# Hybrid decoder layer on one core: another order for weight splits, bank copies and the loading of hidden sums in the MLP

## The reference

```
x = x + gate1 * (concat(attention, retention) @ w_out)
h = rms_norm(x, norm2_g) * (1.0 + scale2) + shift2
x = x + gate2 * (square(relu(h @ w_mlp1)) @ w_mlp2)
```

## Time and profile before

| | |
|---|---|
| median of 3 runs | 1140.83 us |
| profiled execution | 1139.11 us, of which the span is 1137.3 us |
| TensorE busy in the span | 1093.8 us (96%) |
| VectorE busy | 762.2 us (67%) |
| ScalarE busy | 442.0 us (39%) |
| GpSimd busy | 244.0 us (21%) |
| mean granted TensorE clock | 0.985 of full |

### The profile page before, as it was taken

The page is one execution under the profiler, slowest core; times in us unless marked ns, Lnnn a source line. Parts: engine busy times, 40 slices in busy tenths (PEclk is TensorE's granted clock), DMA queues, the critical chain, the costliest instruction groups (busy, mean ns, idle before and its releaser), DMA issues. The chain is left out here.

```text
span 1137.3 us, 14052 instructions
## 1 busy us (share of the span) xinstructions
PE 1093.8 (96%) x5210; PEld 884.9 (78%) x5210; DVE 762.2 (67%) x1206; ACT 442.0 (39%) x746; POOL 244.0 (21%) x219
## 2 busy tenths in 40 slices
PE   5999999999999999997999999999899999999998
PEld 4578877777778988775888888888678788787786
DVE  5673556564546767897676767667986957848752
ACT  6342333354444334662232323233523514426231
POOL 2011000000001105312222323233323223232231
PEclk9899999999999999998999999999999999999999
DMA  9958433332013013103535353537626345336205
GB/s 272 275 163 265 130 123 101 122 101 90 28 38 122 28 33 108 38 0 130 193 113 191 114 190 116 187 120 224 257 95 233 135 148 191 99 117 222 74 1 148
DMA packets 150932, 151.71 MB, mean 133 GB/s; under 512 B 14116, under 2 KB 124880, under 8 KB 147280
## 3 DMA queue, kind: packets, MB, share of 16 engines
q1 hardware_dynamic: 142800, 122.45, 33.4%
q0 software_dynamic: 8064, 28.36, 7.6%
HBM read 113.04 MB, written 37.75 MB: 133 GB/s over the span
## 5 line engine op out<-in xcount | busy, mean ns | idle before, releaser
L739 PE MATMUL ps<-cmb_hi,wm_hi 128*128 128x512 f32 x880 | 350.0, 398 | 23.2 <-DVE wm_lo L1904 8.1
L740 PE MATMUL ps<-cmb_lo,wm_hi 128*128 128x512 f32 x880 | 346.2, 393 | 0.0
L741 PE MATMUL ps<-cmb_hi,wm_lo 128*128 128x512 f32 x880 | 346.1, 393 | 0.0
L739 PEld LDWEIGHTS ps<-cmb_hi,wm_hi 128*128 128x128 f32 x880 | 167.6, 190 | 65.7 <-issue 12.4
L741 PEld LDWEIGHTS ps<-cmb_hi,wm_lo 128*128 128x128 f32 x880 | 167.4, 190 | 35.7
L740 PEld LDWEIGHTS ps<-cmb_lo,wm_hi 128*128 128x128 f32 x880 | 167.7, 191 | 34.6 <-issue 0.5
L739 PE MATMUL ps<-act_hi,w_hi 128*128 128x512 f32 x400 | 162.3, 406 | 3.0 <-DVE act_lo L1682 3.0
L740 PE MATMUL ps<-act_lo,w_hi 128*128 128x512 f32 x400 | 157.1, 393 | 0.0
L741 PE MATMUL ps<-act_hi,w_lo 128*128 128x512 f32 x400 | 157.0, 392 | 0.0
L1392 ACT ACTIVATE wm_hi<-wm_f 128x512 fp32r<-128x512 f32 x128 | 77.2, 627 | 204.7 <-POOL wm_f L709 158.0
L2155 DVE SCALAR_TENSOR_TENSOR x1t<-ps,ada,x1t 128x512 f32<-128x512 f32 x112 | 83.5, 746 | 79.8 <-PE ps L741 79.8
(11 more groups left out here) (200 smaller groups left out, 1406.4 us busy)
## 6 DMA issues: line engine op xcount, KB each, us to landing
raw<-in_w_mlp_dram SPq DMA_DIRECT2D x128, 256.0 KB, 3.9
cmb_f<-h_spill SPq DMA_DIRECT2D x22, 1024.0 KB, 5.3
wada<-in_w_ada_dram POOLq DMA_DIRECT2D x32, 512.0 KB, 5.0
h_spill<-stage SPq DMA_DIRECT2D x16, 768.0 KB, 6.5
w_raw<-in_w_in_dram SPq DMA_DIRECT2D x18, 512.0 KB, 3.9
ada_rows<-in_w_ada_dram SPq DMA_DIRECT2D x16, 512.0 KB, 7.3
h_spill<-stage SPq DMA_DIRECT2D x32, 256.0 KB, 3.2
h_spill<-stage SPq DMA_DIRECT2D x16, 512.0 KB, 6.7
```

Source lines behind the costliest of these rows:

```text
L739: pe.matmul(bank, wh, hi, start=first, stop=False, skip_group_check=onto)
L740: pe.matmul(bank, wh, lo, start=False, stop=False, skip_group_check=onto)
L741: return pe.matmul(bank, wl, hi, start=False, stop=last, skip_group_check=onto)
```

## The change

Nothing is added to or taken from the arithmetic. Instructions are put in another order in four places.

- **First pairs, VectorE.** The splits of pair 1 (S1, A22, S2) stand ahead of, or between, `c12(0)` and the squares of pair 0. `c11(2)` with its square moves from pair 1 to pair 2, behind `last_sum(1)`. The splits A11 and A12 of pair 3 stand directly behind `last_sum(0)`.
- **First pairs, ScalarE and SyncE.** `weight_hi(1, A22)` moves into pair 0. In pair 1 the hi parts of pair 3's A11 and A12 and of pair 2's S3 and S1 stand ahead of `e2(1)`; `e1(2)` moves into pair 2. The load of pair 3's weights waits for the sums of pair 1. The store of b11 of pair 2 moves one pair later, behind that pair's load and two other stores.
- **Change of phase.** T1, T3 and T2 of chunk 0 are loaded before the last sums are stored. On VectorE `e25(15)` and `c22(15)` stand ahead of the split of B11, `last_sum(14)` behind it, and T2 and T1 are split in pair 16. `e2(15)` moves behind the hi parts of T2 and T1.
- **Chunk ends.** In the last pair of a chunk VectorE adds the last product and the first of the next pair before it splits T1. The first pair of a chunk has one order for all four chunks: T3, additions 1 and 2, S4, B22, addition 3, A22, addition 4, NT4, and only then A11 of the next pair.

```diff
@@ -80,19 +80,19 @@
     if AHEAD <= _a < 2 * PAIRS and _w != PAIRS - 1:
         SPLITS += [(_a, A11), (_a, A12)]
     if _w + 1 < 2 * PAIRS:
-        SPLITS += [(_w + 1, _i) for _i in (S3, S1, S2, S4, A22)]
+        SPLITS += [(_w + 1, _i) for _i in ((S3, S1, S2, S4, A22) if _w else (S3, S1, A22, S2, S4))]
...
-UP_SUMS = [("e25", 0), ("c22", 0), ("c11", 1), ("c11", 0), ("c12", 0), ("e25", 1), ("c22", 1), ("c21", 0), ("c11", 2),
-           ("c12", 1), ("c21", 1)]
-SQUARES = [("b22", 0), ("b11", 0), ("b12", 0), ("b21", 0), ("b11", 1), ("b11", 2), ("b22", 1), ("b12", 1)]
+UP_SUMS = [("e25", 0), ("c22", 0), ("c11", 1), ("c11", 0), ("c12", 0), ("e25", 1), ("c22", 1), ("c21", 0), ("c12", 1),
+           ("c21", 1), ("c11", 2)]
+SQUARES = [("b22", 0), ("b11", 0), ("b12", 0), ("b21", 0), ("b22", 1), ("b11", 1), ("b12", 1)]
...
-    SQUARES += [("b21", _p - 1)] + [("b11", _p + 1)] * _more + [("b22", _p), ("b12", _p)]
+    SQUARES += [("b21", _p - 1)] + [("b11", 2)] * (_p == 2) + [("b11", _p + 1)] * _more + [("b22", _p), ("b12", _p)]
 SQUARES += [("b21", PAIRS - 1)]
...
-FIRST_LOADS = (B11, B21, T1, T2, T3, B22, NT4)
...
-        def loads_of(q):
-            return FIRST_LOADS if q == 0 else tuple(range(7))
-
         def piece(q, i, part):
 
-            return 14 * q + 2 * loads_of(q).index(i) + part + 1
+            return 14 * q + 2 * i + part + 1
 
...
@@ -581,8 +577,15 @@
                     sp.wait_ge(s, 16 * CHUNK_PAIRS * (q + 1))
 
             for p in range(PAIRS):
+                if p == PAIRS - 1:
+                    load_in_place(0, T1)
                 sp.wait_ge(s_wlm, SPLIT[p, A22])
+                if p == 1:
+                    sp.wait_ge(s_s, 4 * p + 4)
                 load_pair(p + 2)
+                if p == PAIRS - 1:
+                    load_in_place(0, T3)
+                    load_in_place(0, T2)
                 if p:
                     store_sums(p - 1)
                     store_b21(p - 1)
@@ -591,7 +594,11 @@
                     store_b11(0)
                     continue
                 if p == 1:
+                    store_b22(1)
                     store_b11(1)
+                    continue
+                if p == 2:
+                    store_b11(2)
                 if p + 1 < PAIRS:
                     store_b11(p + 1)
                     if p == PAIRS - 2:
@@ -599,7 +606,7 @@
                         load_in_place(0, B11)
                         load_in_place(0, B21)
                     store_b22(p)
-            for i in FIRST_LOADS[2:]:
+            for i in (B22, NT4):
                 load_in_place(0, i)
 
             for w in range(PAIRS, 2 * PAIRS):
@@ -1501,29 +1508,30 @@
             e2(0)
 
             for p in range(PAIRS):
-                if p == 1:
-                    weight_hi(1, A22)
-                    e5(1)
-                    e2(1)
-                    e1(2)
-                elif p:
+                if p >= 2:
                     weight_hi(p, A22)
+                    if p == 2:
+                        e1(2)
                     if p + 1 < PAIRS:
                         e1(p + 1)
+                if p:
                     e5(p)
                 if p and p + 1 < PAIRS:
                     weight_hi(p + 2, A11)
                     weight_hi(p + 2, A12)
                 weight_hi(p + 1, S3)
                 weight_hi(p + 1, S1)
-                if p >= 2:
+                if p == 0:
+                    weight_hi(1, A22)
+                elif p + 1 < PAIRS:
                     e2(p)
-                if p == PAIRS - 1:
-                    combination_hi(0, T1)
                 weight_hi(p + 1, S2)
                 if p == PAIRS - 1:
                     combination_hi(0, T2)
                 weight_hi(p + 1, S4)
+                if p == PAIRS - 1:
+                    combination_hi(0, T1)
+                    e2(p)
                 if p == PAIRS - 2:
                     combination_hi(0, B11)
                     combination_hi(0, B21)
@@ -2073,30 +2081,28 @@
             weight_lo(1, S3)
             c11(1)
             c11(0)
+            weight_lo(1, S1)
+            weight_lo(1, A22)
             c12(0)
             squared(ST_B22, n_c22(0))
             squared(0, n_c11(0))
+            weight_lo(1, S2)
             squared(ST_T3, n_c12(0))
-            weight_lo(1, S1)
             hidden_sums(0)
-            weight_lo(1, S2)
             weight_lo(1, S4)
-            weight_lo(1, A22)
             e25(1)
             c22(1)
             c21(0)
             squared(ST_B21, n_c21(0))
             last_sum(0)
-            squared(1, n_c11(1))
-            c11(2)
-            squared(0, n_c11(2))
-            squared(ST_B22, n_c22(1))
             weight_lo(3, A11)
             weight_lo(3, A12)
+            squared(ST_B22, n_c22(1))
+            squared(1, n_c11(1))
             weight_lo(2, S3)
+            weight_lo(2, S1)
             c12(1)
             squared(ST_T3, n_c12(1))
-            weight_lo(2, S1)
             weight_lo(2, S2)
             c21(1)
 
@@ -2104,15 +2110,16 @@
                 weight_lo(p, S4)
                 weight_lo(p, A22)
                 hidden_sums(p - 1)
-                squared(ST_B21, n_c21(p - 1))
-                last_sum(p - 1)
                 if p + 1 < PAIRS:
+                    squared(ST_B21, n_c21(p - 1))
+                    last_sum(p - 1)
+                    if p == 2:
+                        c11(2)
+                        squared(0, n_c11(2))
                     c11(p + 1)
                     squared((p + 1) % 2, n_c11(p + 1))
                     weight_lo(p + 2, A11)
                     weight_lo(p + 2, A12)
-                else:
-                    both_lo(0, B11)
                 e25(p)
                 c22(p)
                 if p + 1 < PAIRS:
@@ -2121,8 +2128,10 @@
                     c12(p)
                     squared(ST_T3, n_c12(p))
                 else:
+                    both_lo(0, B11)
+                    squared(ST_B21, n_c21(p - 1))
+                    last_sum(p - 1)
                     both_lo(0, B21)
-                    both_lo(0, T1)
                     weight_lo(p + 1, S3)
                 weight_lo(p + 1, S1)
                 weight_lo(p + 1, S2)
@@ -2160,52 +2169,24 @@
             for w in range(PAIRS, 2 * PAIRS):
                 q, pp = divmod(w - PAIRS, CHUNK_PAIRS)
                 more, ends = w + 1 < 2 * PAIRS, pp == CHUNK_PAIRS - 1 and q + 1 < CHUNKS
-                if w > PAIRS:
+                if pp == 0:
+                    if w == PAIRS:
+                        add_product(w, 0)
+                        both_lo(0, T2)
+                        both_lo(0, T1)
+                    combination_lo(q, T3, 0)
+                    add_product(w, 1)
+                    add_product(w, 2)
+                    combination_lo(q, T3, 1)
                     weight_lo(w, S4)
+                    combination_lo(q, B22, 0)
+                    add_product(w, 3)
+                    combination_lo(q, B22, 1)
                     weight_lo(w, A22)
-                add_product(w, 0)
-                if w == PAIRS:
-                    both_lo(0, T2)
-                elif pp == 0:
-                    both_lo(q, T3)
-                elif more:
+                    add_product(w, 4)
+                    combination_lo(q, NT4, 0)
+                    combination_lo(q, NT4, 1)
                     weight_lo(w + 1, A11)
-                add_product(w, 1)
-                if w == PAIRS:
-                    both_lo(0, T3)
-                elif pp == 0:
-                    weight_lo(w + 1, A11)
-                    combination_lo(q, B22, 0)
-                elif ends:
-                    both_lo(q + 1, B11)
-                elif more:
-                    weight_lo(w + 1, A12)
-                add_product(w, 2)
-                if w == PAIRS:
-                    weight_lo(w, S4)
-                    weight_lo(w, A22)
-                elif pp == 0:
-                    combination_lo(q, B22, 1)
-                    weight_lo(w + 1, A12)
-                elif ends:
-                    weight_lo(w + 1, A12)
-                    both_lo(q + 1, B21)
-                elif w == PAIRS + 1:
-                    next(remains)
-                add_product(w, 3)
-                if w == PAIRS:
-                    both_lo(0, B22)
-                elif pp == 0:
-                    both_lo(q, NT4)
-                elif w == PAIRS + 1:
-                    next(remains)
-                add_product(w, 4)
-                if w == PAIRS:
-                    both_lo(0, NT4)
-                    weight_lo(w + 1, A11)
-                elif w == PAIRS + 1:
-                    next(remains)
-                if w == PAIRS:
                     add_product(w, 5)
                     weight_lo(w + 1, A12)
                     weight_lo(w + 1, S3)
@@ -2213,17 +2194,44 @@
                     add_product(w, 6)
                     weight_lo(w + 1, S2)
                     continue
```

(31 more changed lines are left out.)

## The result

The changed kernel takes 1143.87 us (median of 10 runs, 1141.61 to 1147.66) beside 1140.34 us for the kernel before on the same chip (10 runs, 1139.25 to 1142.05): a ratio of 1.0038 [1.0024, 1.0051], 3.5 us slower. The forecast was 0.4 us faster. The profiled execution of after took 1145.18 us, 6.1 us more than the profiled one of before (1139.11), with a granted clock of 0.984 over a span of 1143.4 us.

What follows compares the result with a forecast made beforehand. TensorE, busy 96%, bounds the kernel; only gaps and lower-clock matmuls can give time. First pairs +0.9, change of phase -1.0, chunk ends +0.5: 0.4 us less, 1140.4 us from the 1140.83 median; range 1132 to 1146.

Steps and rivals of the forecast that it cites:

- First pairs: Pairs 0 to 2: 11.1 us of gaps gone, 5.6 and 4.6 us of new waits, net 0.9 us gained.
- The wait before S4 of pair 1: First pairs: S4 waits for e5(1) behind hidden sums delayed by GpSimd, 3.9 us plus 1.7 tail, 5.6 taken.
- The second: First pairs: S4 of pair 2 waits for the late b11(2) store, 2.9 us plus 1.7 tail, 4.6 in all.
- Change of phase: Pairs 15 and 16: 7.1 us of gaps gone, 8.4 us new, net 1.3 lost, 1.0 lost used.
- The walked gaps: Pair 16: S2 late 1.1 us, S3 0.3, S4 2.0 and 0.3, A22 2.7; with restarts 6.7 us.
- Chunk ends: Three chunk ends: 4.4 us gone against new waits at A22, 0.2 us gained each, 0.5 for three.
- The order of turns at B22: Chunk end: VectorE splits B22's first half before GpSimd's first sum at 895.2; A22's product and second half lose 3.4 us.
- The tail at half its price: Chunk end: slow passes behind the new A22 gap of 2.3 us, a 1.7 us tail counted at half.
- The gap that went: Chunk end: the 2.55 us wait before S2 of pair 20 vanishes with restart and tail, 4.4 us gained.
- The third rival, "the tails all come": Whole kernel: A22 gaps halve the clock, 0.7 us lost per chunk end; 4.3 us slower, 1145 us; chance 0.26.
- The row that decided the sums: Row at 820.00: VectorE and GpSimd take turns, so a GpSimd sum delays VectorE's SBUF work by up to 1.2 us.

Runs made afterwards that it cites:

- e5: In `e5(1)` not a run: ScalarE's copy from PSUM of pair 1, which S4 of pair 1 waits for; no measured time of its own.
- first pairs alone: Kernel before with only the change's new orders for pairs 0 to 2: 1140.87 us beside 1139.51, ratio 1.0004.
- the part alone: Kernel before with only the change of phase edited (loads, splits and additions of pairs 15 and 16): 1139.58 us beside 1139.51, ratio 1.0002.
- Passes in the gap: "ends alone" plus nine unread TensorE passes before the wait for A22 of a chunk's first pair: 1138.86 us beside 1140.27, ratio 0.9991.
- ends alone: Kernel before with only the new order at the three chunk ends: 1144.43 us, ratio 1.0043.
- Sums spread: "ends alone"; second pair's GpSimd sums wait, one for A22's split, the rest for NT4's; product 0 added before S4, A22 splits: 1132.22 us beside 1140.27.
- sums later: "first pairs alone" with GpSimd held before pair 2's sums until pair 0's hidden sums are done: 1137.95 us beside 1140.27, ratio 0.9976.
- all together: First run: kernel before with "sums later", earlier b11 squares, stores and e1(2), and "Sums spread"; change of phase as before: 1127.64 us beside 1139.37.

## Why the prediction was wrong

**First pairs: right in place; the net is near by luck.** The three hidden sums take 1.67 to 1.76 us each and `e5(1)` runs at 524.32 (walked: 524.5):

```profile
524.32 0.60 ACT L1473 ACTIVATE stage<-ps 128x512 f32<-128x512 f32 x1 [8.03 <-DVE stage L2028]
547.53 0.60 ACT L1466 ACTIVATE stage<-ps 128x512 f32<-128x512 f32 x1 [12.21 <-DMA h_spill<-stage]
```

The wait before S4 of pair 1 costs 3.4 us (forecast 3.9) and in this execution had no tail (1.7 counted); in that of "first pairs alone" it had one. The second costs 4.5 us, forecast 2.9. SyncE's queue is as walked, the load at 536.95 and three stores from 539.02, and the last, issued at 542.4, lands after 5.0 us at 547.4, 0.4 us ahead of the forecast. `e1(3)` is where it was expected (547.53). The miss is in when S4 was due: TensorE had nothing to do from 544.1 (its last pass started at 543.91), not from 546.2, since the first wait had cost 2.2 us less. The store came when it did, so what the first wait saved the second lost, and the longer gap had a longer tail (2.7 us). Counted 5.6 and 4.6, measured 3.4 and 7.2: two misses of over 2 us cancel, and 0.3 was gained against 0.9. "First pairs alone", with both tails, lost 0.8 in its profile.

**Change of phase: right.** `c22(15)` ends at 795.43, as walked. The walked gaps 1.1, 0.3, 2.0, 0.3 and 2.7 stand as 1.16, 0.46, 0.72 with 0.90, 0.27 and 2.74 (starts of passes less one pass); 1.4 us were lost in the profile and 1.3 walked, of which 1.0 was used. By medians the part alone cost nothing that can be told.

**Chunk ends: the step that failed.** Forecast, 0.5 gained in three: "VectorE: ... B22 first half 896.1; sum; second half 898.4", and "this gap of 2.3 lies at the edge, so half". Three terms were mis-sized, all in the sum for a chunk end.
- *The order of turns at B22.* The walk had VectorE's first half of B22 start 0.3 us ahead of GpSimd's sum (894.9 and 895.2). In after everything stands 1.3 us later here (the same split pair starts at 881.93 in before and at 883.21 in after). By that the sum came when it was walked and VectorE 0.4 us late: its split of T1, T3 and two additions took a little longer than was added up. The sum came first, at 896.50 against 896.61, so the first half of B22 was held as well, addition 3 was late and S4 waited. The gaps are 0.66 + 0.51 + 2.74 = 3.9 us in place of 3.4, about 0.5 us at each end, 1.6 us in all.
- *The tail at half its price.* The gap was 2.57 us idle where 2.3 was walked, and a tail came behind all three of the profile. "Passes in the gap" measures it: 5.6 us for three, 1.9 each, where 0.85 was counted: 3.1 us in all (2.4 if the tail is taken at the 1.6 to 1.7 us that the traces show).
- *The gap that went.* It was counted at 4.4 us; by the same distances it was 4.26, 4.28 and 4.10: 0.6 us in all.

Together 5.3 us at the chunk ends: 0.5 gained becomes 4.8 lost by this account (4.1 with the smaller tail), 4.8 by the profile and 4.9 [3.3, 6.5] by "ends alone". The third rival, "the tails all come", had this place and mechanism, with 0.7 lost at each end; without the first term it, too, was too low there. It was given 0.26, and its time, 1145, was the nearest, in part by luck: its 2.1 us at the chunk ends were 4.9, and what it took off for the other two parts can't be told from nothing. By their ratios the three parts alone add up to 5.6 us and the whole change to 4.3, which the intervals cover.

**The row that decided the sums held.** "Sums spread" and "sums later" show it from both sides: with no sum beside it a half takes 1.21 us and a hidden sum 0.68, with one 2.3 and 1.7. "SBUF — State Buffer", section "SBUF: two separate sides", of the Trainium skill has the loser blocked for the whole instruction; both runs agree. By the same section the pair of ports goes to whichever starts first, and the trace agrees here too: the sum, 0.11 us ahead, ran its 1.34 us and the split took 2.31. The forecast had the turns right and missed who came first.

**Not settled.** Whether a gap of 2.3 to 3.3 us brings a tail differs between places and executions: none behind 3.25 us at 524.98 in after, one (clock 0.53) behind 3.27 us before the same S4 in "first pairs alone". Over the MLP of the 13 profiles none of 35 gaps of 0.9 to 1.5 us has a tail, one of four of 1.8 to 2.1 (1.82 us, in the first run of "all together"), 17 of 27 of 2.3 to 2.4, all eight of 2.57 and all ten of 3.6 us and more. So a half for a gap of 2.3 us was not far off; the gap that came was longer, and it had a tail each time. That one at 1.82 us:

```profile
524.85 0.47 PE L752 MATMUL ps<-cmb_hi,wm_hi 128*128 128x512 f32 x1 [1.82 <-DVE wm_lo L1917]
525.00:529.00 4.00, 4.00 (x11) 3.13 (x12) 3.90 (x7) 2.42 (x5) 2.10 (x2) 0.57 0.74 281
```

What decides it was not found out. The ten executions of after have mean clocks from 0.981 (1147.5 us) to 0.986 (1141.6 us), so part of their spread of 6 us goes with it. Nor is it known whether the change of phase, left as in before, loses 2 us more because the first pairs are faster or by where the tails happened to fall: two profiles show it, and that of "sums spread", with 2.51 us and no tail at the same place, loses 7.5 us as before did.

## What to carry to other kernels

Before an order of work is tightened on one engine, ask which other engine is released earlier by it and whether the two get in each other's way; a wait that holds the second engine back for a few us can be worth more than the new order: with it, and with one addition moved, 8 us were gained here, and without it 5 were lost. Hold it back by parts: all of it later only moved the wait on by a pair. And price a gap of TensorE with what follows: here 2.6 us of waiting cost 4.5.

## What the runs showed of the hardware

- A gap's tail can be taken away without shortening the wait: nine passes that nothing reads, ahead of the wait, gave back 1.9 us at each place (1138.86 beside 1144.43 us).
- An operation that starts 0.11 us behind one of the other engine waits for nearly the whole of it (2.31 us for 1.22, beside a sum of 1.34).
- The store behind a 1 MB load and two other stores lands 5.0 us after its issue in after and 6.1 us in before, where the median store of its size (256 KB) in before takes 3.2 us.
- A gap of TensorE need not reach 3 us to have passes at the lower clock behind it: 17 of 27 gaps of 2.3 to 2.4 us have 7 or 8 slow passes behind them (1.5 to 1.7 us), none of 35 under 1.5 us has.
